# A fifth expert in the fixed set, and block counts of three and two taken in turn, in a mixture-of-experts stage on one core

## What is computed

```python
grp_prob = softmax(h @ w_rg + b_rg)                 # 4 groups
p_grp, g_sel = top_k(grp_prob, 1)
sel = the 8 expert logits (h @ w_re + b_re) of that group
w_top, i_top = top_k(softmax(sel), 2)               # two experts a token
gates = p_grp * w_top / sum(w_top)
for each of the 32 experts e:                       # w_gu[e]: 1024 x 512, w_dn[e]: 256 x 1024
    g_act, up = split(h @ w_gu[e])
    out += (silu(g_act) * up * combine[:, e]) @ w_dn[e]
return rmsnorm(x + out, norm_final)
```

## Time and profile before

| | us |
|---|---|
| median of 3 runs | 1200.62 |
| lowest and highest | 1192.73, 1200.79 |
| the profiled execution's own time | 1200.39 |
| span of its profile, first to last instruction | 1198.6 |

### The profile page before, as it was taken

How to read it: one execution, slowest core, us unless ns; L and a number is a source line. 1 busy time by engine, 2 the same in 40 slices (tenths; PEclk the granted TensorE clock), 3 DMA queues, 4 the chain that set the end, 5 groups by cost and what they waited for, 6 DMA issues and landing times.

```text
span 1198.6 us, 16494 instructions
## 1 busy us (share of the span) xinstructions
PE 1121.6 (94%) x6487; PEld 618.4 (52%) x6487; DVE 537.9 (45%) x1196; ACT 351.3 (29%) x676; POOL 131.0 (11%) x154
## 2 busy tenths in 40 slices
PE   6999999999999899898799999999999999997886
PEld 5545744444844689875474444456643333332322
DVE  5876333334499544796572222335532121211116
ACT  4114631112676322204664000265201111110004
POOL 2010012220000000001100000132011111211004
PEclk9999999999999999999899999999999999998998
DMA  8111022131022443420114000461369999999938
GB/s 275 43 53 58 21 74 82 53 106 46 25 71 110 179 138 72 170 100 1 75 68 176 0 1 1 146 246 71 133 230 350 403 403 423 420 424 424 404 145 335
DMA packets 65973, 196.35 MB, mean 164 GB/s; under 512 B 24444, under 2 KB 41056, under 8 KB 55392
## 3 DMA queue, kind: packets, MB, share of 16 engines
q1 hardware_dynamic: 59184, 178.25, 39.1%
q0 software_dynamic: 6656, 16.95, 3.7%
q10 hardware_dynamic: 48, 0.01, 0.0%
HBM read 167.38 MB, written 33.05 MB: 167 GB/s over the span
## 4 chain that ended last, share of the span: by engine, by line
PE 75%; DVE 11%; issue 4%; ACT 3%; DMA 1%; POOL 0%; DVEq 0%; SPq 0%; POOLq 0%; ACTq 0%
PE bank L2633 20%; PE bank L1545 13%; PE bank L1601 8%; PE bank L1568 6%; PE bank L1663 2%; PE bank L1616 2%; PE bank L2760 2%; PE bank L805 1%; PE bank L1531 1%; PE bank L916 1%; PE bank L866 1%; PE bank L1683 1%; PE bank L853 1%; PE bank L884 1%; DVE arena L756 1%
## 5 line engine op out<-in xcount | busy, mean ns | idle before, releaser
L2633 PE MATMUL bank<-arena 128*128 128x512 f32 (+3 forms) x1032 | 356.9, 505 | 8.1 <-ACT arena L2137 6.8
L2633 PEld LDWEIGHTS bank<-arena 128*128 128x128 f32 x1032 | 196.2, 192 | 162.7 <-issue 140.7
L1545 PE MATMUL bank<-arena 128*32 128x512 f32 x1344 | 154.4, 612 | 15.6 <-issue 14.6
L1545 PEld LDWEIGHTS bank<-arena 128*32 128x32 f32 x1344 | 47.0, 113 | 118.9 <-issue 118.9
L1601 PE MATMUL bank<-arena 128*128 128x512 f32 x220 | 95.6, 592 | 0.0
L1318 DVE TENSOR_TENSOR arena<-arena,bank 128x256 f32<-128x256 f32 x21 | 8.8, 421 | 161.1 <-ACT arena L1204 126.9
L1568 PE MATMUL bank<-arena 128*32 128x512 f32 x672 | 76.5, 595 | 1.6 <-ACT arena L1208 1.4
L2137 ACT ACTIVATE arena<-bank 128x512 f32<-128x512 f32 (+1 forms) x57 | 28.4, 504 | 165.8 <-PE bank L2633 165.3
L1361 DVE TENSOR_TENSOR arena<-arena,bank 128x512 f32<-128x512 f32 x32 | 22.0, 688 | 101.6 <-PE bank L1601 79.5
L1601 PEld LDWEIGHTS bank<-arena 128*128 128x128 f32 x220 | 41.3, 190 | 49.7 <-issue 49.7
L1204 ACT ACTIVATE arena<-bank 128x256 f32<-128x256 f32 x21 | 8.0, 383 | 168.4 <-PE bank L1545 168.4
(11 more groups left out here) (411 smaller groups left out, 1585.4 us busy)
## 6 DMA issues: line engine op xcount, KB each, us to landing
arena<-in_w_e_gu SPq DMA_DIRECT2D x26, 2048.0 KB, 14.4
arena<-in_w_e_dn SPq DMA_DIRECT2D x32, 1024.0 KB, 15.4
arena<-in_w_in SPq DMA_DIRECT2D x11, 1024.0 KB, 5.2
arena<-y_d SPq DMA_DIRECT2D x8, 1024.0 KB, 11.2
arena<-hz_d SPq DMA_DIRECT2D x4, 1792.0 KB, 8.0
arena<-in_w_e_gu SPq DMA_DIRECT2D x6, 1024.0 KB, 10.0
arena<-in_w_e_gu SPq DMA_DIRECT2D x12, 512.0 KB, 13.4
pk_d<-arena SPq DMA_DIRECT2D x8, 640.0 KB, 2.9
```

The costliest lines, as they stand in the source:

```text
L1545: ins = mm(bank[part, :], hgT[:, k, part], w_gu(es[i] % NB, k), start=(k == 0), stop=(k == KT - 1))
L2633: ins = mm(psum[PROJ_BANKS[u % 3]][0:rows, 0:n], lhs(k), rhs(k), start=(k == 0), stop=(k == kt - 1))
```

## The change

The expert at place 4 becomes fixed: `FIXED` is 5, and it has three blocks. The ranked experts then have one of four blocks at place 5 and, from place 6 on, three and two blocks in turn, 13 times, instead of fourteen of three and then thirteen of two. Both orders have 84 blocks and 21 units, 18 experts of three blocks and 13 of two. Expert 4 is loaded in two parts during the routing: its first two pieces of gate-up weights right behind expert 2, and the third piece with the down weights once the last store to `xn_d` has landed and the router is done. For that, the router's small tiles move from `o_g3` to tiles of earlier stages (`levT`, `lru_w`, `tril_s`), and one one-hot tile moves to `o_tmp`. Since `levT` is also `fin_g`, the load of the final norm's gain moves behind the last expert's load. The pool's constants are written by as many instructions as before.

```diff
-        FIXED = 4
-        CAPS = [3] * FIXED + [4] + [3] * 14 + [2] * 13
+        FIXED = 5
+        CAPS = [3] * FIXED + [4] + [3, 2] * 13
...
-        rt = region(o_g3, o_bc)
+        rt = region(0, (NL + 1) * P, levT[:, :, :].rearrange("p a b -> p (a b)"))
+        ru = region(0, 2 * CT * P, lru_w[:, :, :].rearrange("p a b -> p (a b)"))
...
-        io_i = rt(P).bitcast(i32)
+        io_i = tril_s[:, :].bitcast(i32)
...
-        oh, rtmp = rt(BT * TK, NE), rt(BT, TK, NE)
+        oh, rtmp = ru(BT * TK, NE), ru(BT, TK, NE)
...
-        ohb = [view(o_tmp + (5 + i) * D, BT * TK, P) for i in range(2)]
+        ohb = [view(o, BT * TK, P) for o in (o_tmp + 5 * D, o_tmp)]
...
-        def load_gu(sp, e):
+        def load_gu(sp, e, parts=None):
             expert, j = expert_at(sp, e), e % NB
-            for off, k0, k1 in GU_AT[j]:
+            for off, k0, k1 in parts or GU_AT[j]:
...
-            sp.dma_start(fin_g, a["norm_final"].unsqueeze(0).to_broadcast([P, D])).then_inc(s["t_x2"], 16)
+            load_gu(sp, 4, GU_AT[4][:2])
...
+            sp.wait_ge(s["t_rl"], NT)
+            sp.wait_ge(s["t_slt"], NT)
+            load_gu(sp, 4, GU_AT[4][2:])
+            load_dn(sp, 4)
             sp.wait_ge(s["t_r_dve"], 4)
-            sp.wait_ge(moe["g0"], 16)
-            load_gu(sp, 4)
-            load_dn(sp, 4)
             sp_experts(sp, moe, 0)
...
-            for e, n in ((FIXED + 1, 14), (FIXED + 15, 13)):
-                for i in range(CAPS[e]):
-                    at_b = i * NBL + FIRST[e] + i
-                    nc.gpsimd.iota(ranks_of[:, at_b:at_b + (n - 1) * CAPS[e] + 1:CAPS[e]], [[1, n]], base=e,
-                                   channel_multiplier=0).then_inc(s["consts_i"], 1)
+            pairs = (NE - FIXED - 1) // 2
+            for i in range(5):
+                at_b = (i if i < 3 else i - 3) * NBL + FIRST[FIXED + 1] + i
+                nc.gpsimd.iota(ranks_of[:, at_b:at_b + 5 * pairs - 4:5], [[1, pairs]],
+                               base=FIXED + 1 + (pairs if i >= 3 else 0),
+                               channel_multiplier=0).then_inc(s["consts_i"], 1)
...
         def sp_tail3(sp):
+            sp.dma_start(fin_g, a["norm_final"].unsqueeze(0).to_broadcast([P, D])).then_inc(s["t_x2"], 16)
             pass_end(sp, moe, 0)
```

More of the change, by code:

```diff
@@ L955, in hybrid_trunk, with region @@
         G2, G3 = MT_ + NT, MT_ + 2 * NT
-        def region(start, end):
+        def region(start, end, of=None):
             at = [start]
@@ L965, in take @@
                 assert at[0] <= end, (at[0], end)
-                return view(at[0] - n, *shape)
+                if of is None:
+                    return view(at[0] - n, *shape)
+                t = of[:, at[0] - n:at[0]]
+                if len(shape) == 1:
+                    return t
+                if len(shape) == 2:
+                    return t.rearrange("p (a b) -> p a b", a=shape[0])
+                return t.rearrange("p (a b c) -> p a b c", a=shape[0], b=shape[1])
             return take
         TK = 2
-        FIXED = 4
-        CAPS = [3] * FIXED + [4] + [3] * 14 + [2] * 13
+        FIXED = 5
+        CAPS = [3] * FIXED + [4] + [3, 2] * 13
         assert len(CAPS) == NE
```

## The result

The changed kernel takes 1.0031 times the time of the one before, 95% interval 1.0017 to 1.0046: 3.7 us more on 1197.14 us, the median of 20 runs of before (the changed kernel's median is 1200.2 us, also of 20). One run in each 20 took some 1921 us (its granted clock in the changed kernel was 0.56) and is left out of the ratio. So the change is slower by a third of a per cent. The interval excludes "no change", although the difference is well inside the 1% that the prediction took as the least that could be told.

What follows compares the result with a forecast made beforehand. TensorE and the weight transfers were taken as about equal bounds, with load order deciding. Terms 3.9 - 1.9 + 1.0 + 0.3 = 3.3 us on 1200.39 gave 1203.7 us; range 1194 to 1213.

Steps and rivals of the forecast that it cites:

- Expert 4 leaves the queue: Start of the expert stage: its 3.146 MB leave an idle stretch, nothing behind moves up; 0, bounds 7.5 us won to 0.
- The middle: Transfers from 944 to 980 us fill from 393 to 422 GB/s, so the last transfers land 2.5 us earlier.
- The end: Units 19 and 20: unit 19 waits for place 30, unit 20 starts 3.9 us later; sum 3.3 us later.
- 1.0 us set aside for a slow product: Unit 19's gate-up product may run slow after a longer wait; half of 1.9 us taken as cost.
- 0.3 us for two short waits: End of the stage: 0.3 us added for two short waits at ScalarE's evictions.
- The routing: Early loads land the first xn_d store 2.5 us later, the rest as the first gather starts; 0, bounds 0 to 2 us.
- The final gain: fin_g load behind the last expert, near 1130, read 30 us later; 0, bounds 0 to 1.2 us.
- The rival of slow products in the middle: From unit 11 on, each second unit waits and runs its gate-up product in 9.69 us; 10 us slower, 1213.7; chance 0.10.

Runs made afterwards that it cites:

- late-load run: The changed kernel with only expert 4's load put back behind the first gather, blocks still alternating; ratio 1.0045 (1.0030 to 1.0060) against the kernel before.
- old order with the early load: The changed kernel with the old order of blocks, expert 4 still loaded during the routing; ratio 1.0006 (0.9990 to 1.0021) against the kernel before.

## Why the prediction was right

The time was forecast at 1203.7 from a profiled 1200.39, 3.3 us or 0.28% slower; measured is 0.31%, and 3.1 us in the profiled stage from the first gather on. The mechanism is the one forecast: the transfers fill up in the middle, and unit 19 starts at place 30's landing. That the sum comes out within 0.2 us is partly luck, as its last terms missed both ways. By its steps:

- *Expert 4 leaves the queue: 0.* Right. At most 0.2 us at unit 19 with the alternating order, and a ratio of 1.0006 with the old. Place 5 was issued 8.15 us after unit 0's start, against 7.86 before; nothing moved up.
- *The middle: 2.5 us won.* The window filled as said, to 422 GB/s. Place 31 landed 1128.7 - 878.2 = 250.5 us after unit 0, before 252.3: 1.8 us won of the 2.5. (One reading was loose: 4.99 MB in 11.75 us are 425 GB/s, so by its own figures the first half of the old order stood at the limit and not just under it.)
- *The end.* Place 30 to 31 took 5.4 us, forecast 5.3. Unit 19 was forecast 8.1 us later and came 8.8 later; the difference is the 0.7 us of the step above. Unit 20 was forecast 3.9 us later and came 4.8 later, 0.2 us more, as unit 19's product took 7.09 us. Unit 20 ran in 6.93 instead of 8.77 us, 1.8 us back of 1.9. The 1.0 us set aside for a slow product was not needed beside these 0.2, nor the 0.3 us for two short waits, which had stood in the kernel before too. So 0.9 us too little at unit 20 and 1.3 us too much behind it nearly cancel. In the late-load run, where the slow product did come, the last scatter was 4.8 us later than before instead of 3.3. Sum: 4.8 - 1.8 = 3.0 from unit 0 on, and 0.1 between the first gather and unit 0, 3.1.
- *The routing: 0.* The first store landed 12.9 us after its issue, 2.7 more (2.5 forecast), and delayed nothing that the runs show. The rest of expert 4, issued from 866.69, had landed at 867.06 + 6.7 = 873.8, which is 1.6 us after the first gather was issued, not just before it; that gather landed in 4.4 us instead of 4.3.
- *The final gain: 0.* It landed in 7.4 us, at 1137.9, long before its use.
- *The rival of slow products in the middle* saw what would happen, but not its price. Four of them cost 1.9 + 1.8 + 1.9 + 1.8 = 7.4 us of TensorE's time, and the windows around them moved 417 to 426 GB/s all the same, up to 1102 us: they only ate the next waits. (From there to 1126 us, where the loads end, it was 405.) The Trainium skill, TensorE: Matmul & The Clock Gate, section "HAM oscillation — how this bites in real kernels", says that a wait for transfers between two groups of matmuls can slow the clock for the group behind it, time after time. The trace agrees for the waits of 3.64, 3.26 and 4.37 us, each with a slow product behind it. In this stage those products don't add to the time: with only the last four places changed they are still there, and the time is that of before.

What the prediction did not see is how finely the last places decide: 3.2 us at unit 20 lie between two orders of the last four, and 2.5 us between two places of one expert.

## What to carry to other kernels

When a stream of weights and TensorE are near equal bounds, a load taken out of the stream is worth nothing if the stream then stands still for want of free memory: look at the GB/s of that stretch, and at when the next load may be issued, before counting its bytes. Even demand fills the stream, but the end of the stage is set by the first unit that needs one of the last loads, counted with all the work that still follows it; give the last units experts of their own. Putting the expert with most work per byte ahead of them was worth 2.5 us at unit 20 in the one pair of orders tried here. Waits and slow products in the middle cost nothing here while the windows around them were full.

## What was not expected of the hardware

A gate-up product after a wait of 2.38 us ran in 7.09 us, one after 3.26 us in 8.77, one after 5.22 us in 10.00 (old order with the early load) where 6.87 is usual. A wait of 2.22 us was also followed by a down product of 5.34 instead of 3.57 us, but its wait began 13 us behind a product that had run slow itself. With half of the down weights left out of the kernel before, a wait of 2.32 us was followed by a gate-up product of 8.70 us, at a granted clock of 0.50 from 1106.25 to 1108 us, and no product of the stage ahead of it had run slow. So waits of 2.32 and 2.38 us came out on either side, and the length of the wait alone does not tell. The down-weight load of 1.049 MB behind place 17's took 28.4 us from issue to landing, and these were mostly queue: the same size lands in 6.7 us in the routing.
